# Two of the eight modulation products moved forward: into the first attention's seventh block and between two token tiles of the second attention's projections

## The chip, the cores and the metric

The kernel runs on one NeuronCore of a Trainium2 chip. The time is device microseconds (us) of one execution, from launch to the end of the output, and the number to predict is the median over several executions of the changed kernel. Beside it a profiled execution gives a trace, with the start and duration of every instruction on the five engines: TensorE (PE, with its weight loads as PEld), VectorE (DVE), ScalarE (ACT), GpSimd (POOL) and SyncE (SP, which issues nearly all DMAs).

## The reference

The program computes two transformer blocks on 512 tokens of width 1024. The first block has two attentions on the same input and a layer of 16 experts; the second has an mLSTM mixer and a gated convolution. Only the part around the change matters here:

```python
# first block, 512 tokens, D = 1024
o_a = window_gqa(q_a, k_a, v_a, rel_bias, sink)          # 8 heads, windows of 128 tokens
q  = rms_norm(c_q)  @ w_qb                                # 384 -> 8 x 96
kv = rms_norm(c_kv) @ w_kvb                               # 256 -> 8 x 128
o_b = softmax(q_nope k_nope + q_rot k_rot) v              # full attention, 8 heads
...
# second block: one row of 6 x 1024 numbers for c, one for c_ctx
mod   = silu(c)     @ w_mod + b_mod                       # w_mod is 1024 x 6144
mod_c = silu(c_ctx) @ w_mod + b_mod
```

The second block's modulation rows do not depend on the first block, so the kernel computes them while the first block's attentions run.

## The kernel before

**Order of work.** Every engine has one instruction stream written out by hand; engines wait for one another on semaphores (`wait_ge(*at(step, key))` waits for a named step, `then_inc(*inc(step, key))` marks it). Nothing is reordered by a planner.

**First attention.** It runs in eight blocks b = 0 to 7 (four blocks of 128 query tokens, two groups of heads). In the loop on TensorE block b does: the scores of block b+1 (`a_scores`, L520), for some blocks a modulation step (`mod_rows`, L530), the turning of block b's probabilities (L552, called At here), and the product with the values (L561, called Ao). The probabilities that At turns come from VectorE and ScalarE (exponential, L1167; scaling, L1649). "Seventh block" is b = 6.

**Second attention, front.** For each of four token tiles t TensorE makes the q projection (L574) and the kv projection (L580). ScalarE and VectorE follow tile by tile: copies out of PSUM (VectorE: L1663 for q, L1670 for kv), squares, norms, and the rotation, whose last instruction is L1060 and marks `qk` for the tile. Then TensorE waits for `qk` of tile 3, turns heads 0 and 1 (`b_heads`, L600), does the last modulation step, and begins the scores (`b_scores`, L433 to L435). ScalarE and VectorE split the turned heads in two parts (r_bh and r_bl, L1707).

**Modulation.** The product has K = 1024, cut in eight steps k of 128 rows. A step reads 128 x 6144 weights as two halves, so there are 16 loads m = 0 to 15 of 1536 KB each; `mod_rows(k)` waits for load 2k, does its six products, waits for load 2k+1 and does six more, and marks `pe_mod` after each half. The results of the eight steps are added up in three PSUM banks, which ScalarE copies out after `pe_mod` 15 (`modrow`, L1068), in front of its first exponential of the second attention (L1227).

The loads go into a ring of three buffers, so load m is issued by SyncE only when half m-3 has been multiplied (L2251, L2252):

```python
if m >= 3:
    sp.wait_ge(*at("pe_mod", m - 3))
sp.dma_start(w_mod[:, m % 3, :], ...)
```

Behind load 15 SyncE issues w_o (L2253), and after `pe_mod` 15 the first four expert loads (L2262).

Of the kernel before, what the change touches and what calls it, by code (L numbers as in the profile page):

```python
# [19 lines left out]
KD = D // P  # L20
# [72 lines left out]
class Marks:  # L93
# [14 lines left out]
    def inc(self, name, key=0, by=1):  # L108
        shared = SEM_OF.get(name, name)
        self.count[shared] = self.count.get(shared, 0) + by  # L110
        self.here[name, key] = self.count[shared]
        return self.sem(name), by

    def at(self, name, key=0):
        return self.sem(name), self.value(name, key)
# [37 lines left out]
def program(nc, I, out, known):  # L153
# [6 lines left out]
    with ctx:  # L160
# [31 lines left out]
        def bank(b, n=HALF):  # L192
            return PS[:, b * HALF:b * HALF + n]
# [220 lines left out]
        def _(pe):  # L414
# [10 lines left out]
            def nb(key, *freed_by, banks=8):  # L425
                b = turn[0] % banks
                turn[0] += 1
                bank_of[key] = claim(b, *freed_by)
                return b
# [12 lines left out]
            for t in range(NT):  # L442
                pe.wait_ge(*at(f"x_in{t}"))
                half, odd = divmod(t, 2)
                for k in range(KD):
                    b = 4 * half + k // 2
# [16 lines left out]
            for half in range(2):  # L463
# [5 lines left out]
                for k in range(KD):  # L469
# [13 lines left out]
                    for i in range(6):  # L483
                        t, c, kk = (i // 3, i % 3, k) if half == 0 else (2 + k // 4, (6 * (k % 4) + i) // 8, (6 * k + i) % 8)
# [8 lines left out]
            for j in range(10):  # L493
                freed = ("qT_" + "da"[j % 2], j) if j < 4 else ("kz", 3) if j == 4 else ("cT", j - 5)
                b = nb(("T", j), freed)
# [14 lines left out]
            def keys(n):  # L510
                return max(0, n - 1), min(NT - 1, n + 1)

            def a_scores(b):
                n, g = divmod(b, 2)
                lo, hi = keys(n)
                for i in range(4):
                    h = 4 * g + i
                    x = nb(("As", b, i), ("As", (b, i)), banks=5)
                    r = slice(64 * (h % 2), 64 * (h % 2) + 64)
                    pe.matmul(bank(x, (hi - lo + 1) * P), qTa[r, h // 2, n * P:(n + 1) * P],  # L520
                              kz[r, g, lo * P:(hi + 1) * P], start=True, stop=True).then_inc(*inc("pe_As", (b, i)))

            def mod_rows(k):

                for half in range(2):
                    m = 2 * k + half
                    pe.wait_ge(*at(f"w_mod{m % 3}", m))
                    for j2 in range(6):
                        r, j = divmod(6 * half + j2, 4)
                        mm = pe.matmul(PS[32 * j:32 * j + 32, (5 + r) * HALF:(6 + r) * HALF], csil[:, k, :],  # L530
                                       w_mod[:, m % 3, j2 * HALF:(j2 + 1) * HALF], start=(k == 0), stop=(k == KD - 1),
                                       skip_group_check=True)
                    mm.then_inc(*inc("pe_mod", m))
# [6 lines left out]
            for b in range(8):  # L540
                n, g = divmod(b, 2)
                lo, hi = keys(n)
                nk = hi - lo + 1
                if b < 7:
                    a_scores(b + 1)
                if b in (1, 2, 4, 5, 7):
                    mod_rows((1, 2, 4, 5, 7).index(b))
                for i in range(4):
                    x = nb(("At", b, i), ("ptA_" + "da"[i % 2], (b, i)), banks=5)
                    pe.wait_ge(*at("Ap", (b, i)))  # L550
                    for kk in range(nk):
                        tr = pe.transpose(bank(x)[:, kk * P:(kk + 1) * P], pA[:, 4 * (b % 2) + i, kk * P:(kk + 1) * P], ident)  # L552
                    tr.then_inc(*inc("pe_At", (b, i)))
                x = nb(("Ao", b), ("oTa", b), banks=5)
                for i0 in (0, 2):
                    for i in (i0, i0 + 1):
                        pe.wait_ge(*at("ptA_" + "da"[i % 2], (b, i)))
                    for kk in range(nk):
                        for i in (i0, i0 + 1):
                            o = PS[64 * (i % 2):64 * (i % 2) + 64, x * HALF + (i // 2) * P:x * HALF + (i // 2 + 1) * P]  # L560
                            mm = pe.matmul(o, zr[:, lo + kk, g * AD:(g + 1) * AD], ptA[:, i, kk * P:(kk + 1) * P],  # L561
                                           start=(kk == 0), stop=(kk == nk - 1), skip_group_check=True)
                mm.then_inc(*inc("pe_Ao", b))
# [6 lines left out]
            for t in range(NT):  # L570
# [6 lines left out]
                for c in range(2):  # L577
# [2 lines left out]
                        mm = pe.matmul(bank(x), cqT[:, 3 + k, t * P:(t + 1) * P], w_kvb[:, k, c * HALF:(c + 1) * HALF],  # L580
                                       start=(k == 0), stop=(k == 1))
                    mm.then_inc(*inc("pe_kv", (t, c)))
            for k in range(5, KD - 1):
                mod_rows(k)

            def turn_mod():

# [1783 lines left out]
```

## Time and profile before

| | us |
|---|---|
| median of 3 runs | 1560.69 |
| lowest and highest | 1559.26 and 1561.72 |
| the profiled execution: its time | 1559.61 |
| the profiled execution: its span in the trace | 1557.8 |

The span runs from the first to the last instruction in the trace; the execution's own time is 1.8 us more. Times in the rows below are counted from the start of the span. In the table of windows, PEclk is the TensorE clock that was granted as a share of full speed: 1.00 is 2.4 GHz and 0.50 is 1.2 GHz.

### The profile page before, as it was taken

Reading aid. Unit: us, or ns where it says so; the run is one execution under the profiler, and the core shown is the slowest. Engines: PE = TensorE matmul, PEld = TensorE weight load, DVE = VectorE, ACT = ScalarE, POOL = GpSimd, SP = SyncE. Lnnn points to the kernel's source line nnn. Section 1 sums busy time; section 2 is a strip of 40 time slices with the busy share of each in tenths; the row PEclk is TensorE's granted clock in tenths of the full one; section 3 lists DMA queues with packets and bytes.
Section 4 is the critical chain, followed back from the end, with each engine's and each line's share of the span. In section 5 each row is a group of like instructions: output and inputs, shape, how many; then the busy total and the mean of one; then the engine's idle time right before and its main releaser. Section 6 shows DMA issues by size and latency. Waiting matters only on the chain.

```text
span 1557.8 us, 17583 instructions
## 1 busy us (share of the span) xinstructions
PE 1459.2 (94%) x7133; PEld 956.3 (61%) x7133; DVE 616.2 (40%) x1188; ACT 490.8 (32%) x904; POOL 69.4 (4%) x96
## 2 busy tenths in 40 slices
PE   8988988998999999999996999988898999999998
PEld 6855466454433433333323899966686888888886
DVE  5366666334122222122115542125675443254325
ACT  6355376331001101100103412357734333123321
POOL 2000000000000000000001200000001101000100
PEclk9989999999999999999998999989999999999999
DMA  7477350427999999999995122140021332233211
GB/s 231 81 306 280 131 208 1 149 104 283 423 420 422 421 421 421 421 421 422 421 421 201 41 89 75 55 162 1 10 86 54 109 108 76 87 108 108 101 35 54
DMA packets 82738, 310.27 MB, mean 199 GB/s; under 512 B 7188, under 2 KB 43309, under 8 KB 55906
## 3 DMA queue, kind: packets, MB, share of 16 engines
q1 hardware_dynamic: 80656, 305.34, 50.2%
q10 hardware_dynamic: 1202, 2.15, 1.2%
q0 software_dynamic: 800, 1.66, 0.3%
q8 instruction: 57, 0.93, 0.2%
q14 instruction: 23, 0.19, 0.0%
HBM read 303.35 MB, written 5.78 MB: 198 GB/s over the span
## 4 chain that ended last, share of the span: by engine, by line
PE 73%; DMA 14%; DVE 6%; ACT 5%; issue 1%; SPq 0%; DVEq 0%; ACTq 0%
PE ps L433 13%; PE ps L434 13%; PE ps L435 13%; PE ps L805 13%; DMA sb<-in_w_gate 5%; DMA sb<-in_w_up 5%; PE ps L663 4%; DMA sb<-in_w_down 2%; PE ps L932 1%; PE ps L757 1%; DMA raw<-in_a_w_in 1%; ACT sb L1068 1%; PE ps L530 1%; PE ps L574 1%; PE ps L620 1%
## 5 line engine op out<-in xcount | busy, mean ns | idle before, releaser
L805 PE MATMUL ps<-sb 128*64 128x512 f32 x1536 | 352.5, 599 | 15.7 <-DMA sb<-in_w_gate 5.4
L805 PEld LDWEIGHTS ps<-sb 128*64 128x64 f32 x1536 | 102.9, 136 | 222.2 <-issue 178.6
L1068 ACT ACTIVATE sb<-ps 128x512 f32<-128x512 f32 (+4 forms) x176 | 90.7, 530 | 342.5 <-PE ps L757 88.3
L434 PE MATMUL ps<-r_fl,r_top 128*128 128x512 f32 x344 | 135.1, 393 | 0.0
L435 PE MATMUL ps<-r_act,r_low 128*128 128x512 f32 x344 | 134.8, 392 | 0.0
L433 PE MATMUL ps<-r_act,r_top 128*128 128x512 f32 x344 | 134.3, 390 | 0.0
L2096 DVE TENSOR_TENSOR r_low<-raw,r_top 128x2048 fp32r<-128x2048 f32 x33 | 74.2, 2289 | 78.7 <-ACT r_top L1068 78.7
L1874 DVE TENSOR_TENSOR sb<-sb,ps 128x512 f32<-128x512 f32 x64 | 43.7, 687 | 139.6 <-PE ps L794 139.6
L433 PE MATMUL ps<-r_low,r_h 128*128 128x256 f32 x288 | 82.5, 287 | 1.0 <-ACT sb L1068 1.0
L1068 ACT ACTIVATE r_top<-raw 128x2048 fp32r<-128x2048 f32 x33 | 61.4, 1907 | 69.7 <-PE ps L435 69.7
L434 PE MATMUL ps<-r_low,r_h 128*128 128x256 f32 x288 | 82.3, 286 | 0.0
L434 PE MATMUL ps<-r_low,r_mid 128*128 128x512 f32 x208 | 80.9, 389 | 0.0
L433 PEld LDWEIGHTS ps<-r_act,r_top 128*128 128x128 f32 x344 | 64.6, 188 | 14.7
L434 PEld LDWEIGHTS ps<-r_fl,r_top 128*128 128x128 f32 x344 | 64.6, 188 | 14.5
L435 PEld LDWEIGHTS ps<-r_act,r_low 128*128 128x128 f32 x344 | 64.6, 188 | 14.1
L435 PE MATMUL ps<-r_low,r_hl 128*128 128x256 f32 x256 | 73.2, 286 | 0.0
L1330 ACT ACTIVATE sb<-ps 128x512 f32<-128x512 f32 x16 | 9.6, 597 | 197.0 <-PE ps L805 197.0
L435 PE MATMUL ps<-r_top,r_mid 128*128 128x512 f32 x176 | 68.5, 389 | 0.0
L433 PE MATMUL ps<-r_top,r_mid 128*128 128x512 f32 x176 | 68.5, 389 | 0.0
L433 PEld LDWEIGHTS ps<-r_low,r_h 128*128 128x128 f32 x288 | 56.1, 195 | 1.8 <-issue 1.7
L663 PE MATMUL ps<-sb 128*128 128x512 f32 x128 | 56.3, 594 | 0.9 <-ACT sb L1068 0.9
L434 PEld LDWEIGHTS ps<-r_low,r_h 128*128 128x128 f32 x288 | 56.1, 195 | 0.0
(396 smaller groups left out, 2382.4 us busy)
## 6 DMA issues: line engine op xcount, KB each, us to landing
sb<-in_w_gate SPq DMA_DIRECT2D x64, 1024.0 KB, 25.3
sb<-in_w_up SPq DMA_DIRECT2D x64, 1024.0 KB, 26.0
sb<-in_w_down SPq DMA_DIRECT2D x64, 1024.0 KB, 26.4
sb<-in_w_mod SPq DMA_DIRECT2D x16, 1536.0 KB, 9.1
raw<-in_f_w_up SPq DMA_DIRECT2D x22, 1024.0 KB, 7.6
raw<-in_a_w_in SPq DMA_DIRECT2D x12, 1024.0 KB, 5.4
raw<-in_f_w_down SPq DMA_DIRECT2D x5, 2048.0 KB, 7.8
raw<-in_w_in SPq DMA_DIRECT2D x3, 1440.0 KB, 16.5
```

The source lines that it names most:

```text
L433: pe.matmul(o, a_hi, b_hi, start=first, stop=False)
L434: pe.matmul(o, a_hi, b_lo, start=False, stop=False)
L435: return pe.matmul(o, a_lo, b_hi, start=False, stop=last)
L530: mm = pe.matmul(PS[32 * j:32 * j + 32, (5 + r) * HALF:(6 + r) * HALF], csil[:, k, :], w_mod[:, m % 3, j2 * HALF:(j2 + 1) * HALF], start=( ...
L574: mm = pe.matmul(bank(x, 384), cqT[:, k, t * P:(t + 1) * P], w_qb[:, k, c * 384:(c + 1) * 384], start=(k == 0), stop=(k == 2))
L620: mm = pe.matmul(PS[64 * e:64 * e + 64, x * HALF:x * HALF + 256], vb[:, kk, h * VD:(h + 1) * VD], pT[g % 2][e][:, kk, :], start=(kk == 0), ...
L663: mm = pe.matmul(bank(x), oT[:, k, t * P:(t + 1) * P], w_o[:, k, hf * HALF:(hf + 1) * HALF], start=(k == 4 * part), stop=(k == 4 * part + 3))
L757: mm = pe.matmul(bank(6 + hf), onehot[:, t, :], part[t][:, hf * HALF:(hf + 1) * HALF], start=(t == 0 and part is h2hi), stop=(t == NT - 1 ...
L805: mm = pe.matmul(PS[64 * hf:64 * hf + 64, b * HALF:(b + 1) * HALF], lhsT(k), ring[c % RINGN][:, kk, hf * HALF:(hf + 1) * HALF], start=(k = ...
L1068: return act_(o, i_, ACT.Identity, bias=bias, scale=scale)
L1874: ve.tensor_tensor(o, o, bank(scatter_bank(i, n)), ALU.add).then_inc(*inc("x_add", (i, n)))
L2096: ve.tensor_tensor(w_lo(q, o, 2048), w_raw(q, o, 2048), w_hi(q, o, 2048).bitcast(F32), ALU.subtract).then_inc(*inc("wlo", (q, half)))
```

## The change

Steps k = 0 to 4 of the modulation stood in blocks 1, 2, 4, 5 and 7 of the first attention, and steps 5 and 6 behind the last projection. Now steps 0 to 5 stand in blocks 1, 2, 4, 5, 6 and 7, and step 6 stands behind the projections of token tile 1. Step 7 stays behind `b_heads`. The loads are the same and in the same order, and no other engine's code is changed.

```diff
-                if b in (1, 2, 4, 5, 7):
-                    mod_rows((1, 2, 4, 5, 7).index(b))
+                if b in (1, 2, 4, 5, 6, 7):
+                    mod_rows((1, 2, 4, 5, 6, 7).index(b))
...
                     mm.then_inc(*inc("pe_kv", (t, c)))
-            for k in range(5, KD - 1):
-                mod_rows(k)
+                if t == 1:
+                    mod_rows(6)
```

On TensorE, in block 6 of the first attention (L520 is here the scores of block 7, L552 and L561 the At and Ao of block 6, L530 a modulation step):

```order
 L561 MATMUL ps<-sb 64x128 x12
 L520 MATMUL ps<-sb 128x256 x4
+L530 MATMUL ps<-sb 32x512 x12
 L552 MATMUL ps<-sb 128x128 x8
 L561 MATMUL ps<-sb 64x128 x8
```

A step of twelve products, which is now k = 4, has come in between the scores of block 7 and the At of block 6; the step in block 7 stays in its place and is now k = 5.

On TensorE, in the projections of the second attention (L574 and L580 are the q and kv products of one token tile, L600 is `b_heads`; the rows begin with token tile 1):

```order
 L574 MATMUL ps<-sb 128x384 x6
 L580 MATMUL ps<-sb 128x512 x4
+L530 MATMUL ps<-sb 32x512 x12
 L574 MATMUL ps<-sb 128x384 x6
 L580 MATMUL ps<-sb 128x512 x4
 L574 MATMUL ps<-sb 128x384 x6
 L580 MATMUL ps<-sb 128x512 x4
-L530 MATMUL ps<-sb 32x512 x24
 L600 MATMUL ps<-sb 96x128 x16
 L530 MATMUL ps<-sb 32x512 x12
```

The 24 products of steps 5 and 6 have gone from between the last projection and `b_heads`; twelve of them, step 6, stand behind token tile 1.

## Rows read from the trace of the kernel before

**Rows 1.** The page: its span, and TensorE's busy time.

```profile
span 1557.8 us, 17583 instructions
PE 1459.2 (94%) x7133; PEld 956.3 (61%) x7133; DVE 616.2 (40%) x1188; ACT 490.8 (32%) x904; POOL 69.4 (4%) x96
```

**Rows 2.** Timeline of TensorE, blocks 6 and 7: start, length, instructions, idle before.

```profile
137.00 1.13 PE L520 MATMUL ps<-sb 64*128 64x256 f32 x8
140.53 1.20 PE L552 MATMUL ps<-sb 128*128 128x128 f32 x8 [2.39 <-DVE sb L1649]
142.13 1.98 PE L561 MATMUL ps<-sb 128*64 128x128 f32 x16 [0.40 <-DVE sb L1654]
144.03 3.36 PE L530 MATMUL ps<-sb 128*32 128x512 f32 x24
147.33 1.09 PE L552 MATMUL ps<-sb 128*128 128x128 f32 x8
```

**Rows 3.** SyncE: issues of loads 7 and 8, then of loads 9 and 10.

```profile
125.73 1.22 SPq L2252 DMA_DIRECT2D sb<-in_w_mod  x2
...
133.18 1.22 SPq L2252 DMA_DIRECT2D sb<-in_w_mod  x2
```

**Rows 4.** Time from issue to landing: loads 7 and 8 together; load 9; load 10.

```profile
DMA to landing us min/median/max: 6.2/7.6/9.1
...
DMA to landing us min/median/max: 8.5/8.5/8.5
...
DMA to landing us min/median/max: 11.2/11.2/11.2
```

**Rows 5.** Timeline of TensorE, from the projections to the scores of the second attention.

```profile
149.63 4.14 PE L574 MATMUL ps<-sb 128*128 128x384 f32 x12
...
179.04 4.49 PE L530 MATMUL ps<-sb 128*32 128x512 f32 x36
187.36 3.63 PE L530 MATMUL ps<-sb 128*32 128x512 f32 x12 [3.83 <-DMA sb<-in_w_mod]
190.91 2.97 PE L600 MATMUL ps<-sb 128*96 128x128 f32 x16
193.82 2.82 PE L530 MATMUL ps<-sb 128*32 128x512 f32 x24
196.57 0.50 PE L433 MATMUL ps<-r_bh,r_bh 96*128 96x512 f32 x1
```

**Rows 6.** SyncE: issue of loads 13 and 14; below it the landing of load 13.

```profile
181.00 1.22 SPq L2252 DMA_DIRECT2D sb<-in_w_mod  x2
...
DMA to landing us min/median/max: 6.3/6.3/6.3
```

**Rows 7.** Timeline of VectorE: tile 0's first copy, tile 2's copies, tile 3's last instruction.

```profile
153.81 0.56 DVE L1663 COPY sb<-ps 128x384 f32<-128x384 f32 x1 [2.60 <-PE ps L574]
...
172.01 0.55 DVE L1663 COPY sb<-ps 128x384 f32<-128x384 f32 x1
...
174.40 0.42 DVE L1670 COPY sb<-ps 128x256 f32<-128x256 f32 x1
...
188.69 0.28 DVE L1060 TENSOR_TENSOR sb<-sb 128x128 f32<-128x128 f32 x1
```

**Rows 8.** Windows of one us, columns as in the first line.

```profile
core 0: us, PE busy (x) PEld busy (x) DVE busy (x) ACT busy (x) POOL busy (x), PEclk, DMA share, GB/s
142.00:143.00 1.00, 0.87 (x8) 0.90 (x10) 1.00 (x2) 0.25 (x1) 0.00 (x0) 0.50 0.84 356
187.00:188.00 1.00, 0.64 (x4) 0.20 (x8) 0.97 (x5) 0.00 (x0) 0.00 (x0) 0.50 0.98 418
192.00:193.00 1.00, 1.00 (x7) 0.95 (x6) 0.24 (x1) 0.79 (x2) 0.00 (x0) 0.50 1.09 467
193.00:194.00 1.00, 1.00 (x12) 0.79 (x14) 0.89 (x2) 1.00 (x2) 0.00 (x0) 0.98 0.84 356
```

**Rows 9.** Timeline of ScalarE behind the last modulation step.

```profile
196.69 1.57 ACT L1068 ACTIVATE sb<-ps 128x512 f32<-128x512 f32 x3 [1.94 <-PE ps L530]
...
199.57 0.69 ACT L1227 ACTIVATE sb<-ps,sb 128x512 f32<-128x512 f32 x1
```

## The prediction, made before the changed kernel ran

> **What bounds the kernel now.** I read the page first: TensorE is busy 94% of a span of 1557.8 us [rows 1], so in most of the program what moves a TensorE instruction moves the end. Then I read the timeline of TensorE around the edit, the idle times in brackets above all, and for each idle time the engine that ended it. Two stretches matter. In block 6 the scores of block 7 end at 137.00 + 1.13 = 138.13, and TensorE is idle for 2.39 us until VectorE has scaled the probabilities [rows 2]. That looks like a free place for products. The second is the tail behind the projections: steps 5 and half of 6 begin at 179.04, then TensorE idles 3.83 us for load 13, which was issued only at 181.00, when the first half of step 5 was done, and landed 6.3 us later [rows 6], the second half of step 6 takes from 187.36 to 190.91, `b_heads` follows at 190.91, step 7 at 193.82, and the scores begin at 196.57 [rows 5]. ScalarE begins to copy the modulation rows at 196.69, when step 7 ends, and begins its first exponential only at 199.57 [rows 9]. So the end of step 7 releases the whole second attention, and everything behind it. I therefore follow that one moment, 196.57, and take its shift as the shift of the end.
>
> The third view is the clock. In the windows it stands at 0.50 (1.2 GHz) at 142, and again from 187 until it is back near 1.00 (2.4 GHz) at 193 [rows 8]; both times TensorE had been idle shortly before. The reader should see that the tail before costs not only the wait of 3.83 us: the half step behind it takes 190.91 - 187.36 = 3.55 us, and a whole step (24 records, two for each product) takes only 196.57 - 193.82 = 2.75 us at full clock [rows 5].
>
> **The change part by part.**
>
> *Removed from the tail.* Steps 5 and 6 took 190.91 - 179.04 = 11.87 us of TensorE's time, wait included [rows 5]. But this is not what is gained. `b_heads` also waits for the rotation of tile 3 on VectorE, which ends at 188.69 + 0.28 = 188.97 [rows 7]. So if nothing else moved, `b_heads` could start 190.91 - 188.97 = 1.94 us earlier and no more; with some 0.1 us for the signal, 1.8. The stall goes from a DMA to VectorE.
>
> *Step 4 in block 6.* It can start at 138.1. Its first half needs load 8, issued second in the pair at 125.73 and landed 9.1 us after its own issue, near 135.7 [rows 3, 4]: there. Its second half needs load 9, issued at 133.18 and landed 8.5 us later, at 141.7 [rows 3, 4]. So the free 2.39 us are spent mostly waiting for a load. The ring explains it: load 9 is issued when the first half of step 3 is multiplied, and nothing of the change makes that earlier. A half step on its own took 3.55 us at low clock, so I take half of that, 1.8 us, at full clock. At of block 6 starts at 141.7 + 1.8 = 143.5 at full clock and 145.2 at the low one, in place of 140.53. Ao follows 1.6 us later (142.13 - 140.53) and took 1.98 us, so block 6 ends between some 146.5 and 148.5, in place of 144.03 [rows 2].
>
> *Step 5 in block 7.* Load 10 was issued second of its pair, near 134.07, and landed 11.2 us later, at 145.3, that is 3.6 us behind load 9 [rows 3, 4]; it is there. Load 11 needs the first half of step 4, which now ends at about 139.9, so SyncE issues it near 140.3, behind loads 9 and 10 in a queue that is full. It lands one load's time after load 10: 145.3 + 3.7 = 149.0. The second half of step 5 then runs from 149.0 to 150.8. If block 6 ran late at low clock, the two halves run together and end about there too (147.8 + 2.75 = 150.6). At of block 7 started at 147.33 before [rows 2], so everything behind it starts 3.3 us later, 3.5 at most of this working. Here is the price: the step moved into a gap of 2.39 us waits for transfers that were not asked for early enough.
>
> On the price of a load there is a figure to weigh. The trace gives 3.6 to 3.8 us for 1536 KB in a full queue [rows 4]. The Trainium skill, "DMA: Bandwidth & Descriptors", section "Specifications", gives some 358 GB/s as the limit from HBM for one core; as an estimate from that page a load would take 4.4 us and load 11 land at 149.7, so the sum would be 0.7 us more. The row decides, and it is nearer to the page's other figure, 435 GB/s for the fabric.
>
> *Step 6 between tiles 1 and 2.* Its loads 12 and 13 are issued near 145 and 148 and land before 160 even by the slowest time of a load here, 11.2 us; step 6 starts near 149.63 + 3.3 + 2 x 7.35 = 167.6, since the four tiles took (179.04 - 149.63)/4 = 7.35 us each [rows 5]. It costs 2.75 us of TensorE at full clock. Does this delay VectorE, which now sets the end of this stretch? Its tile takes (172.01 - 153.81)/2 = 9.1 us in the mean of the first two [rows 7], TensorE's 7.35, so TensorE has run ahead. Tile 2's q products ended at 149.63 + 2 x 7.35 + 4.14 = 168.5 and VectorE took them at 172.01: 3.5 us of cover for 2.75. The kv products ended at 149.63 + 3 x 7.35 = 171.7 and VectorE took them at 174.40: 2.7 us of cover for 2.75, even. I take 0.1 us. Without that cover the step would cost its full 2.75.
>
> *The tail after.* VectorE's end moves with the start of the projections: 188.97 + 3.3 + 0.1 = 192.4, and `b_heads` starts near 192.5. TensorE is done with the projections near 179.04 + 3.3 + 2.75 = 185.1 and idles some 7.4 us, longer than the 3.83 us before, so the clock is low again when `b_heads` starts. `b_heads` took 2.91 us at low clock (193.82 - 190.91) and takes the same, until 195.4. Before, the clock rose at about 193, as step 7 began; now it will rise somewhere in step 7 or behind it. At full clock step 7 takes 2.75 us, at low clock 5.5. Before, TensorE had worked for 5.7 us (from 187.36 to the rise at 193.0) when the clock rose [rows 5, 8]; the low stretch at 142 was over after less. If it rises at 196.5, step 7 ends at 198.7; after 5.7 us, at 198.2, it ends at 199.6; if not in time, at 200.9. Against 196.57 that is +2.1, +3.0 and +4.3. I take +2.4, between the first two.
>
> *Else.* SyncE issues w_o near 170 and not at 184, in an idle queue, and nobody waited for it; I count nothing. The expert loads behind `pe_mod` 15 move with it. The sum, at the end of step 7: 1.94 us of the tail's 11.87 can be kept (-1.94), blocks 6 and 7 cost +3.3, VectorE +0.1 and the signal +0.1, which puts `b_heads` 1.56 us later; the clock in step 7 costs a further +0.84. Net +2.4 us: 1557.8 + 2.4 = 1560.2 of span. The execution's own time is 1.8 us above its span and 1.1 us below the median, so on the median 1560.69 + 2.4 = 1563.1; I say 1563.0.
>
> **Bounds.** Low: if loads 9 to 11 follow load 8 without the slip (135.7 + 3 x 3.7 = 146.8), the second half of step 5 ends at 148.9 by its own work before it, the shift there is 1.6 us, and with the clock rising early step 7 ends at 188.97 + 1.7 + 2.9 + 2.75 = 196.3, -0.2 us. High: TensorE's idle in blocks 6 and 7 brings a low stretch just when load 11 is in. Before, such a stretch cost Ao and step 4 about 0.9 and 0.6 us; 1.5 more, with step 7 wholly at low clock, gives 4.3 + 1.5 = +5.8 us. To both I add some half us for the spread of the three runs.
>
> **The rivals.** A change of 0.2%, 3.1 us, is about what a measurement of this kernel can tell from none.
>
> Forecast, 0.66: the waits for loads 9 and 11 eat the gap, VectorE takes over the tail, and it ends at +0.5 to +3.1 us (1561.2 to 1563.8).
>
> Slower, 0.28, the other side: the clock. Its place is step 7, its price is up to 2.75 us, and it decides if the clock rises later than some 5.8 us after `b_heads` starts: then step 7 ends behind 199.7, more than 3.1 us late. For it speaks the rise before after 5.7 us of work, and an idle time twice as long; against it that the rise at the first low stretch came sooner. It gives 1564 to 1566.5. The Trainium skill, "TensorE: Matmul & The Clock Gate", section "What's actually happening", says that the low clock is the default, that activity releases it, and that the chip looks on a schedule of its own that does not start with the kernel. By that rule a longer idle before `b_heads` speaks against this change, and the place of the rise differs between executions. The trace agrees so far that both low stretches follow idle times; no row here shows the schedule.
>
> The change does what its name promises, 0.06: load 11 lands early, the delay in block 7 is 1.6 us or less, and the clock is high in half of `b_heads`, which saves 1.4 of its 2.91 us. Then step 7 ends at 188.97 + 1.7 + 1.5 + 2.75 = 194.9, -1.6 us: 1559.1, and only with luck elsewhere below 1557.6, 0.03 of it. Against it stands VectorE's 188.97, which the edit can't move forward.
>
> It changes nothing: the tail's gain and blocks 6 and 7 cancel within half a us; this is the forecast's low end, and it is counted there and in the case above.
>
> **How the numbers follow.** Slower by more than 0.2%: 0.28. Faster by more: 0.03. The rest, 0.69, within. The range of 8 in 10 runs from 1560.0 (the low bound with the spread of the runs) to 1566.5 (the high bound).
>
> **What the changed profile would show.** In block 6 TensorE waits some 2 us in front of L530 for w_mod, in place of VectorE's 2.39 us. In block 7 a second wait for w_mod, or none if block 6 ran at low clock, and the projections start near 153. The wait for load 13 is gone, and a wait of about 7 us for VectorE stands before L600, which starts near 192.5; ScalarE's copies of the modulation rows start at 198.5 to 201. I am wrong if the projections start before 151.5 (load 11 is faster than the queue says), if L600 starts more than 3.5 us behind the projections' own shift (step 6 starves VectorE), or if stretches far behind the edit move by more than this shift.

## The result and the profile after

The changed kernel takes 1565.15 us in the median of 20 runs (1560.67 to 1569.16), the kernel before 1561.25 us in 20 runs beside them. The ratio is 1.0024, with a 95% interval of 1.0017 to 1.0032: slower by 3.9 us, a little more than the 0.2% that I had called the limit of a measurement. It lies inside the range of 1560.0 to 1566.5, 2.15 us above the value given; 0.56 us of this is the kernel before, whose median is 1561.25 over 20 runs and was 1560.69 over three.

The page has the same number of instructions as before [rows 1], and 3.6 us more span:

```profile
span 1561.4 us, 17583 instructions
PE 1458.0 (93%) x7133; PEld 954.9 (61%) x7133; DVE 616.3 (39%) x1188; ACT 491.4 (31%) x904; POOL 67.5 (4%) x96
```

TensorE is busy a little less (1458.0 us against 1459.2) in a longer span, so over the whole span the loss is waiting; a busy time also holds what a low clock adds, and low stretches differ from profile to profile, as shown further on. Timeline of TensorE in the changed kernel, from the scores of block 7 to the scores of the second attention; it answers to [rows 2, 5]:

```profile
136.80 1.13 PE L520 MATMUL ps<-sb 64*128 64x256 f32 x8
137.86 1.91 PE L530 MATMUL ps<-sb 128*32 128x512 f32 x12
141.74 3.33 PE L530 MATMUL ps<-sb 128*32 128x512 f32 x12 [1.97 <-DMA sb<-in_w_mod]
145.01 1.31 PE L552 MATMUL ps<-sb 128*128 128x128 f32 x8
146.51 1.09 PE L561 MATMUL ps<-sb 128*64 128x128 f32 x16 [0.19 <-ACT sb L1068]
147.53 3.49 PE L530 MATMUL ps<-sb 128*32 128x512 f32 x24
150.95 1.09 PE L552 MATMUL ps<-sb 128*128 128x128 f32 x8
...
153.25 4.14 PE L574 MATMUL ps<-sb 128*128 128x384 f32 x12
...
168.06 2.78 PE L530 MATMUL ps<-sb 128*32 128x512 f32 x24
...
193.01 3.65 PE L600 MATMUL ps<-sb 128*96 128x128 f32 x16 [7.37 <-DVE sb L1060]
196.59 2.81 PE L530 MATMUL ps<-sb 128*32 128x512 f32 x24
199.32 0.50 PE L433 MATMUL ps<-r_bh,r_bh 96*128 96x512 f32 x1
```

Read the brackets first. The idle time of block 6 is still there, 1.97 us, but it now ends with a load and not with VectorE, and it stands in the middle of step 4. Step 5 hides its wait inside a stretch: 24 records take 3.49 us in place of 2.8. The wait of 3.83 us for load 13 is gone from the tail, and 7.37 us for VectorE stand there.

SyncE's issues of loads 9 and 11, each with its time to landing below it:

```profile
132.97 0.33 SPq L2252 DMA_DIRECT2D sb<-in_w_mod  x1
...
DMA to landing us min/median/max: 8.7/8.7/8.7
...
139.81 0.33 SPq L2252 DMA_DIRECT2D sb<-in_w_mod  x1
...
DMA to landing us min/median/max: 9.2/9.2/9.2
```

Load 9 lands at 141.7 and load 11 at 149.0, the two moments that hold TensorE. VectorE, which answers to [rows 7]:

```profile
157.43 0.56 DVE L1663 COPY sb<-ps 128x384 f32<-128x384 f32 x1 [2.59 <-PE ps L574]
...
175.63 0.55 DVE L1663 COPY sb<-ps 128x384 f32<-128x384 f32 x1
...
178.38 0.42 DVE L1670 COPY sb<-ps 128x256 f32<-128x256 f32 x1 [0.27 <-PE ps L580]
...
192.67 0.28 DVE L1060 TENSOR_TENSOR sb<-sb 128x128 f32<-128x128 f32 x1
```

The first copy is 3.62 us later than before and the last rotation 3.98, so VectorE's own stretch has grown by 0.36 us. Between them stands a wait of 0.27 us for tile 2's kv products, behind step 6; before, this copy had no wait in front of it. The windows of one us show the clock, as [rows 8] did:

```profile
189.00:190.00 1.00, 0.00 (x0) 0.00 (x0) 0.68 (x4) 0.22 (x1) 0.00 (x0) 0.93 0.00 0
195.00:196.00 1.00, 1.00 (x6) 0.96 (x5) 0.90 (x2) 0.83 (x2) 0.00 (x0) 0.50 0.00 0
196.00:197.00 1.00, 1.00 (x8) 0.40 (x10) 0.89 (x2) 0.83 (x2) 0.00 (x0) 0.65 0.00 0
197.00:198.00 1.00, 1.00 (x16) 0.31 (x12) 0.89 (x2) 0.38 (x1) 0.00 (x0) 1.00 0.00 0
```

It fell just before 190, ahead of `b_heads`, stayed at 0.50 through it, and rose at 196.7, as step 7 began.

Profiles of one kernel begin this stretch at times that differ by up to 1.9 us, though nothing in front of it was edited. So I count from the start of the scores of block 7 (137.00 before [rows 2], 136.80 after): to the projections 12.63 us before and 16.45 after (+3.82), to `b_heads` 53.91 and 56.21 (+2.30), to the scores of the second attention 59.57 and 62.52 (+2.95).

One thing must be known before the tables are read. In front of the projections the kernel before and four of the experiments have the same code in the same order, and yet their profiles need 12.63, 12.18, 11.16, 12.62 and 11.17 us to the projections. The difference is the clock in blocks 6 and 7. With step 4 in block 7 and the same idle time of 2.39 us, this profile (of the split steps, below) has no low stretch there: Ao takes 1.09 us where it took 1.98 [rows 2], and the step 2.78 where it took 3.36.

```profile
140.90 1.20 PE L552 MATMUL ps<-sb 128*128 128x128 f32 x8 [2.39 <-DVE sb L1653]
...
143.53 2.78 PE L530 MATMUL ps<-sb 128*32 128x512 f32 x24
```

So up to 1.5 us in the column of the projections, and in every column behind it, is this clock and no effect of an edit. What the tail does by itself is read from the projections to `b_heads`, which the table gives as a column of its own.

### The profile page after: what moved, and what is told of

Same layout as the page of the kernel before. It is cut to its first block, busy times and chain, and to the rows that moved or that the text cites. A ratio compares the mean times of both kernels' runs of the same rounds, so it can differ in the third digit from the quotient of the medians.

```text
span 1561.4 us, 17583 instructions
## 1 busy us (share of the span) xinstructions
PE 1458.0 (93%) x7133; PEld 954.9 (61%) x7133; DVE 616.3 (39%) x1188; ACT 491.4 (31%) x904; POOL 67.5 (4%) x96
## 3 DMA queue, kind: packets, MB, share of 16 engines
q10 hardware_dynamic: 1202, 2.15, 1.2%
## 4 chain that ended last, share of the span: by engine, by line
PE 71%; DMA 16%; DVE 6%; ACT 5%; issue 1%; SPq 0%; DVEq 0%; ACTq 0%
PE ps L433 13%; PE ps L434 13%; PE ps L435 13%; PE ps L805 11%; DMA sb<-in_w_gate 7%; DMA sb<-in_w_up 5%; PE ps L663 4%; DMA sb<-in_w_down 2%; PE ps L932 2%; DMA raw<-in_a_w_in 1%; PE ps L757 1%; ACT sb L1068 1%; PE ps L620 1%; PE ps L530 1%; PE ps L574 1%
```

## The experiments

My theory: in blocks 6 and 7 TensorE waits for loads that the ring asks for too late; VectorE takes over the tail, so the wait that goes there brings 1.9 us at most; and the longer idle time in front of `b_heads` keeps the clock low. The rivals: the placement between the tiles costs, or the 2.75 us of products ahead of the projections themselves. Three columns of the table are us from the scores of block 7 in each profile, the fourth is the time from the projections to `b_heads`, and the last is the ratio to the kernel before with its 95% interval.

| kernel | projections | b_heads | scores | projections to b_heads | ratio |
|---|---|---|---|---|---|
| before | 12.63 | 53.91 | 59.57 | 41.28 | 1 |
| changed | 16.45 | 56.21 | 62.52 | 39.76 | 1.0024 (1.0017 to 1.0032) |
| changed, again | 16.06 | 55.80 | 62.09 | 39.74 | 1.0023 (1.0011 to 1.0035) |
| tiles only | 12.18 | 51.94 | 58.07 | 39.76 | 0.9982 (0.9972 to 0.9992) |
| blocks only | 16.00 | 55.40 | 61.56 | 39.40 | 1.0012 (1.0000 to 1.0025) |
| light loads | 11.18 | 50.95 | 57.49 | 39.77 | 0.9988 (0.9975 to 1.0000) |
| busy gap | 15.75 | 55.52 | 60.11 | 39.77 | 1.0001 (0.9989 to 1.0013) |
| ring of four | 12.29 | 52.04 | 58.78 | 39.75 | 0.9987 (0.9974 to 0.9999) |
| ring of four, step 7 early | 12.31 | 52.06 | 57.35 | 39.75 | 0.9985 (0.9974 to 0.9997) |
| split steps | 11.16 | 51.82 | 56.09 | 40.66 | 0.9980 (0.9970 to 0.9990) |
| tiles only, busy | 12.62 | 52.38 | 56.97 | 39.76 | 0.9983 (0.9974 to 0.9993) |
| split steps, rows first | 11.17 | 51.83 | 54.73 | 40.66 | 0.9993 (0.9983 to 1.0004) |

**Tiles only: no step in block 6.**

```diff
-                if b in (1, 2, 4, 5, 6, 7):
-                    mod_rows((1, 2, 4, 5, 6, 7).index(b))
+                if b in (1, 2, 4, 5, 7):
+                    mod_rows((1, 2, 4, 5, 7).index(b))
...
-                if t == 1:
-                    mod_rows(6)
+                if t in (1, 3):
+                    mod_rows(5 + t // 2)
```

> The blocks of the first attention are as in the kernel before (step 4 in block 7), and steps 5 and 6 stand behind token tiles 1 and 3 of the projections. Theory (the price of the change is paid in blocks 6 and 7, by waits for loads 9 and 11): projections start at 149.6 as before; load 11 lands near 153 and load 13, asked for near 166, near 172, so no half step waits; VectorE's last rotation ends near 189.0, b_heads starts at 189.1 with some 4 us of idle time before it, the clock is low in it, and the scores start near 195 to 196 (196.57 before, 199.32 in the changed kernel). Time about 1 to 2 us below the kernel before. Rival (the placement between tiles itself costs): VectorE's end moves by 2 us or more and the time is that of the changed kernel, +2 to +4.

Measured 1559.3 us, ratio 0.9982. TensorE's timeline of the tail:

```profile
149.05 4.14 PE L574 MATMUL ps<-sb 128*128 128x384 f32 x12
...
188.81 3.48 PE L600 MATMUL ps<-sb 128*96 128x128 f32 x16 [4.67 <-DVE sb L1060]
192.23 2.78 PE L530 MATMUL ps<-sb 128*32 128x512 f32 x24
194.94 0.50 PE L433 MATMUL ps<-r_bh,r_bh 96*128 96x512 f32 x1
```

That is 2.8 us below the kernel before, more than the 1 to 2 expected. No wait for a load is left. `b_heads` starts 1.97 us earlier than before by the table, but 0.45 of it is already there at the projections, where nothing was edited: the clock in block 6. The tail itself gained 1.52 us (41.28 to 39.76), of the 1.94 that VectorE's end allows. The steps between the tiles are therefore not free, as the next run shows. With the blocks left alone the kernel is faster than before; with them edited, and a ring of three, it is slower.

**Blocks only: step 6 behind the last tile.**

```diff
-                if t == 1:
+                if t == 3:
                     mod_rows(6)
```

> Steps 0 to 5 in blocks 1, 2, 4, 5, 6, 7 as changed, step 6 behind the last projection and not between tiles 1 and 2. Theory: projections start at 153.2 as in the changed kernel, VectorE's last rotation ends 0.3 us earlier than there (192.7 against 192.95, since the kv products of tile 2 are no longer late), step 6 ends near 185.7 and b_heads waits some 7 us for VectorE all the same; time that of the changed kernel within 0.5 us, +3 to +4 on the kernel before. Rival (step 6 between the tiles is the cost): 2 to 3 us faster than the changed kernel.

Measured 1564.26 us, ratio 1.0012: 1.9 us above the kernel before, where 3 to 4 was expected. That is below the changed kernel's 1.0024 by 1.9 us, nearly the rival's 2 to 3, but the intervals overlap and the times can't decide it. Both waits for loads stand open here, since the clock stayed high in block 6:

```profile
142.77 1.91 PE L530 MATMUL ps<-sb 128*32 128x512 f32 x12 [1.38 <-DMA sb<-in_w_mod]
...
150.26 1.91 PE L530 MATMUL ps<-sb 128*32 128x512 f32 x12 [1.43 <-DMA sb<-in_w_mod]
...
193.81 3.51 PE L600 MATMUL ps<-sb 128*96 128x128 f32 x16 [7.21 <-DVE sb L1060]
```

The projections come 3.37 us late and `b_heads` 1.49, so in the profile nearly all of the price is there without the placement between the tiles. What that placement adds stands in the column from the projections to `b_heads`: 39.40 us here, and 39.74 to 39.77 in the eight profiles in which one whole step stands behind tile 1 and none behind tile 2. It costs 0.36 us, not the rival's 2 to 3.

**Light loads: loads 9, 10 and 11 cut to a quarter.**

```diff
-                sp.dma_start(w_mod[:, m % 3, :], wm[:, m // 2, (m % 2) * 3072:(m % 2 + 1) * 3072])...
+                n = 768 if m in (9, 10, 11) else 3072
+                sp.dma_start(w_mod[:, m % 3, 0:n], wm[:, m // 2, (m % 2) * 3072:(m % 2) * 3072 + n])...
```

> The changed kernel with loads 9, 10 and 11 cut to a quarter of their columns (384 KB in place of 1536 KB), so these weights are left out of the result; same products, same order, same waits. Theory (the loads are late): no wait for w_mod in blocks 6 and 7 beyond 0.5 us, the At of block 6 starts near 140.7 and the projections start at 148.5 to 149.5 in place of 153.25; b_heads starts near 188.5 to 189 and the scores near 195; time 3 to 5 us below the changed kernel, at or just below the kernel before. Rival (the products themselves, 2.75 us more of TensorE's work ahead of the projections, are the price): projections start at 152 or later and the time stays 2 us or more above the kernel before.

Measured 1560.79 us, ratio 0.9988. Blocks 6 and 7 with the same products and quick loads:

```profile
139.15 2.78 PE L530 MATMUL ps<-sb 128*32 128x512 f32 x24
...
144.24 2.78 PE L530 MATMUL ps<-sb 128*32 128x512 f32 x24
```

The rest of these weights is left out; the products are all there. Both steps take their plain 2.78 us with no idle time, and the projections start 5.3 us earlier than in the changed kernel (11.18 against 16.45). They also start 1.45 us earlier than in the profile before, but that is the clock again: the two profiles of the unedited blocks without a low stretch stand at 11.16 and 11.17. Against those, a whole step more in the gap costs nothing. So the products themselves are not the price; the gap in block 6 would have hidden step 4 if its load had been there. The time is below the changed kernel by 0.0036 of 1561, 5.6 us, a little more than the 3 to 5 expected.

**Busy gap: eight products of no use in front of b_heads.**

```diff
+            x = turn[0] % 5
+            for m in owner.get(x, ()):
+                pe.wait_ge(*at(*m))
+            for _ in range(8):
+                pe.matmul(bank(x), ident, w_qb[:, 0, 0:HALF], start=True, stop=True)
             pe.wait_ge(*at("qk", 3))
```

> The changed kernel with eight extra products of 512 columns (ident by w_qb into the PSUM bank that b_heads takes next; their result is overwritten) in the idle time before b_heads, 6.9 us of work in 7.4 us. Theory (part of the price is the low clock behind that idle time): the clock stays at 1.00 through b_heads and step 7, b_heads takes 2.1 us in place of 3.58, the scores start near 197.9 in place of 199.32, and the time is 1.5 us below the changed kernel, more if in most of its executions the clock rises only within step 7. Rival (the clock in this place costs nothing that lasts): the time is that of the changed kernel within 0.5 us.

Measured 1562.34 us, ratio 1.0001. TensorE's timeline and, in a second fence, the window around it:

```profile
186.05 7.03 PE L636 MATMUL ps<-sb 128*128 128x512 f32 x16
193.59 1.95 PE L600 MATMUL ps<-sb 128*96 128x128 f32 x16 [0.51 <-DVE sb L1065]
195.47 2.78 PE L530 MATMUL ps<-sb 128*32 128x512 f32 x24
198.18 0.50 PE L433 MATMUL ps<-r_bh,r_bh 96*128 96x512 f32 x1
```

```profile
186.00:195.00 9.00, 8.49 (x30) 4.27 (x29) 5.95 (x18) 2.57 (x7) 0.00 (x0) 1.00 0.03 8
```

The same 16 turnings take 1.88 us until step 7 (193.59 to 195.47) in place of 3.58 (193.01 to 196.59), and the clock is 1.00 throughout. So work added in a wait makes the kernel faster, here by 1.70 us from `b_heads` to step 7 (the 2.41 us at the scores include 0.70 from in front of the projections). The ratio falls by 0.0023, 3.6 us, with an uncertainty of some 2 us, and the two intervals don't meet; the low clock in this place costs 1.7 us in the profile, and the times agree with that or more.

**Ring of four: the loads asked for half a step earlier.**

```diff
-        w_mod = sb(0, 3, 3072)
+        w_mod = [SB[:, o:o + 3072] for o in (0, 3072, 6144, W_O)]
...
-                if m >= 3:
-                    sp.wait_ge(*at("pe_mod", m - 3))
+                if m >= 4:
+                    sp.wait_ge(*at("pe_mod", m - 4))
...
+            sp.wait_ge(*at("pe_mod", 15))
             sp.dma_start(w_o, ...)
```

> The changed kernel with a ring of four buffers for the loads in place of three (the fourth lies where w_o goes later, so w_o is loaded after step 7); nothing is left out. Theory (loads 9 and 11 are late because they are asked for late): load 9 is asked for near 126 and lands near 136, load 11 is asked for near 134 and lands before 146; no wait of more than 0.5 us in blocks 6 and 7; from the scores of block 7 to the scores of the second attention it takes 57 to 58 us, as with the light loads (57.5), in place of 62.5; time 2 us below the kernel before. Rival (the queue is full in this stretch and an earlier request lands no earlier): load 11 lands near 149 again, and the time is that of the changed kernel.

Measured 1560.11 us, ratio 0.9987. SyncE's issues of loads 9 and 11 and their landing:

```profile
126.66 0.33 SPq L2252 DMA_DIRECT2D sb<-in_w_mod  x1
...
DMA to landing us min/median/max: 9.1/9.1/9.1
...
134.10 0.33 SPq L2252 DMA_DIRECT2D sb<-in_w_mod  x1
...
DMA to landing us min/median/max: 11.0/11.0/11.0
```

Load 9 lands at 135.8 and load 11 at 145.1, 6 and 4 us earlier than in the changed kernel, and the projections start 4.2 us earlier. The rival (a full queue, so no earlier landing) falls: asked for 6.3 us earlier, load 9 also lands 5.9 us earlier, so it was the ring and not the queue that had made it late. For load 11 the queue takes a part back: asked for 5.7 us earlier, it needs 11.0 us in place of 9.2 and lands 3.9 earlier. Step 5 therefore still waits: it took 3.90 us (143.19 to 147.03), 1.1 more than the plain 2.78 and more than the half us that I had allowed. The stretch to the scores took 58.78 us where I expected 57 to 58; the rest of the difference is step 7, which took 3.16 us since the clock rose only within it, 4.5 us behind the start of `b_heads`. The time is 2.0 us below the kernel before, as expected. The edit also moves w_o behind step 7, which was not tried by itself.

**Ring of four with step 7 in front of b_heads.**

```diff
                 if t == 1:
                     mod_rows(6)
+                if t == 3:
+                    mod_rows(7)
...
             b_heads(1, banks=5)
-            mod_rows(KD - 1)
```

> Ring of four as in the run beside it, steps 4 and 5 in blocks 6 and 7 and step 6 behind tile 1 as changed, and step 7 behind tile 3 in place of behind b_heads. Theory: projections start near 149.5 or earlier, VectorE's end is not late by more than 0.1 us, TensorE idles some 4.5 us before b_heads, which starts near 189 at low clock (3 to 3.6 us); the scores start 4 us earlier than before, at 192 to 193; time 4 to 5 us below the kernel before, the fastest of all. Rival (ScalarE's chain behind b_heads takes over): only 2 to 3 us below.

Measured 1559.79 us, ratio 0.9985: 2.3 us below and not 4 to 5; 2 to 3 was the rival's. TensorE's timeline and, in a second fence, the windows show two causes:

```profile
195.66 0.77 PE L433 MATMUL ps<-r_bh,r_bh 96*128 96x512 f32 x1 [1.65 <-DVE r_bl L1708]
```

```profile
190.00:191.00 1.00, 0.63 (x3) 0.61 (x4) 0.31 (x2) 0.00 (x0) 0.00 (x0) 0.50 1.01 410
...
194.00:195.00 1.00, 0.01 (x1) 0.00 (x0) 0.89 (x2) 0.95 (x2) 0.00 (x0) 0.50 1.02 410
...
202.00:203.00 1.00, 1.00 (x9) 0.85 (x8) 1.00 (x3) 0.22 (x1) 0.00 (x0) 0.96 0.99 410
```

With step 7 gone from behind `b_heads`, TensorE idles a second time, at 194, for 1.65 us until VectorE has split the turned heads: that much of the rival is true. And the clock stays at 0.50 until 202, so the first fifteen products of the scores, from 195.66 to the turning at 202.14, take 6.5 us where the changed kernel needs some 3.7. By the scores this kernel is 2.2 us ahead of the one before, by the first turning only 0.4.

**Split steps: all of the modulation in front of b_heads, with the old ring.**

```diff
-            for k in range(5, KD - 1):
-                mod_rows(k)
+                if t == 1:
+                    mod_rows(5)
+                if t == 2:
+                    mod_rows(6, (0,))
+                if t == 3:
+                    mod_rows(6, (1,))
+                    mod_rows(7)
...
             b_heads(1, banks=5)
-            mod_rows(KD - 1)
```

The edit is against the kernel before; the second argument of `mod_rows` picks the halves.

> Blocks of the first attention as before (step 4 in block 7); step 5 behind token tile 1, the first half of step 6 behind tile 2, its second half and all of step 7 behind tile 3, so nothing of the modulation stands behind b_heads any more. Theory (step 7 is on the path only because it stands behind b_heads, and the idle time before b_heads lowers the clock): projections start at 149 to 149.6, load 15 is asked for near 176.5 and lands near 183, TensorE is done with step 7 near 188; VectorE's last rotation is 0.5 to 1 us late (189.5 to 190), because 4.65 us of work stand before tile 3's kv products and only 3.8 are covered; b_heads starts near 190 at full clock, and the scores start near 193, 3.5 us earlier than before (196.57). Time 3 to 4.5 us below the kernel before. Rival (ScalarE's row copies and table load are the bound, whatever TensorE does): the first exponential moves by less than 2 us and so does the time.

Measured 1560.1 us, ratio 0.9980, 3.1 us below the kernel before.

```profile
182.90 4.49 PE L530 MATMUL ps<-sb 128*32 128x512 f32 x36
189.20 1.95 PE L605 MATMUL ps<-sb 128*96 128x128 f32 x16 [1.81 <-DVE sb L1064]
193.47 0.47 PE L433 MATMUL ps<-r_bh,r_bh 96*128 96x512 f32 x1 [2.31 <-DVE r_bl L1711]
...
198.58 0.60 PE L649 MATMUL ps<-sb 128*128 128x128 f32 x4
```

The scores start 3.48 us earlier, of which 1.47 are the clock in blocks 6 and 7, where nothing was edited, and 2.01 the tail. A wait of 2.31 us that step 7 had covered comes to light in front of them, and behind it the clock is low from 194 to 198. The rival is out: the first exponential comes 4.8 us earlier (57.81 us behind the scores of block 7 in place of 62.57).

**Split steps, rows copied first, scores from bank 5.**

```diff
-            b_q(0)
-            b_q(1)
             for r in range(3):
                 eng.wait_ge(*at("pe_mod", 15))
                 copy(modrow[:, r, :], bank(5 + r))...
+            b_q(0)
+            b_q(1)
...
+            turn[0] = 5
             for u in range(4):
                 b_scores(u)
```

> The kernel of the split steps (nothing of the modulation behind b_heads), where the first scores started only at 193.47, 2.3 us after b_heads, behind the last of VectorE's four r_bl parts. Two edits: ScalarE copies the modulation rows ahead of its parts of heads 0 and 1, and the scores begin at PSUM bank 5 in place of bank 4. Theory (the first scores took the bank in which the last turned head still lay, a wait that step 7 covered before): the scores start 1 to 1.5 us earlier against the start of b_heads (2.9 us behind it in place of 4.3), the first turning of probabilities about 1 us earlier, and the time is 0.5 to 1 us below the split steps, 3.5 to 5 below the kernel before. Rival (the scores wait for the heads themselves): no change against the split steps.

Measured 1560.06 us, ratio 0.9993.

```profile
189.10 1.95 PE L605 MATMUL ps<-sb 128*96 128x128 f32 x16 [1.82 <-DVE sb L1065]
192.00 0.47 PE L433 MATMUL ps<-r_bh,r_bh 96*128 96x512 f32 x1 [0.95 <-DVE r_bl L1712]
...
195.79 0.63 PE L650 MATMUL ps<-sb 128*128 128x128 f32 x4
...
212.86 1.05 PE L634 MATMUL ps<-sb 128*128 128x1 f32 x8 [1.99 <-ACT sb L1232]
```

The mechanism was as expected: the scores start 2.9 us behind `b_heads` in place of 4.3, and the first turning follows at 195.79, 6.7 us behind `b_heads` in place of 9.4. But nothing of it lasts. A wait of 1.99 us stands in front of `out_squares` (L634), which takes the fixed bank 7, and behind it the clock is at 0.50 from 215 to 218, which costs some 1.6 us more; the whole is no faster than the split steps. That the new order of banks makes this wait is read from the code and wasn't tried by itself.

**Tiles only with five such products in the gap** (the busy gap's edit with `range(5)`).

> The kernel of the tiles only (steps 5 and 6 behind token tiles 1 and 3), with five extra products of 512 columns (ident by w_qb, overwritten later) in the 4.66 us of idle time before b_heads. Theory (the low clock behind that idle time costs what b_heads takes more than 2 us): b_heads starts near 188.8 as without them, takes 1.95 us in place of 3.4, the scores start near 193.5 in place of 194.9, and the time is 1.5 us below the tiles only, some 3 to 5 us below the kernel before. Rival (the clock's price here is not kept to the end): the same time as the tiles only.

Measured 1558.94 us, ratio 0.9983 against 0.9982 without them. At the scores the gain is there, 1.10 us by the table (56.97 against 58.07; the projections came 0.44 later in this profile); in the times it isn't, though the intervals would allow 1 us. The profiles hold one hint. Both kernels with products of no use have a low stretch near 240 that costs 1.65 us, and neither of the kernels that they were made from has it. The kernel before has it too, with no such products, so this is no proof, and it stays open.

**The changed kernel again.**

> The changed kernel once more, beside the others on the same chip. Loads 9 and 11 land near 141.7 and 149 again and the projections start at 153 to 154; the clock is low in b_heads and may rise up to 2 us later or earlier than in the first profile, which would move the start of the scores against the end of b_heads' wait by as much; time 3 to 5 us above the kernel before.

Measured 1565.88 us, ratio 1.0023. The projections 3.43 us late, the scores 2.52. A second run gives the same loss by the same stations.

## Why the prediction was right, and where it was off

*Blocks 6 and 7, +3.3.* Right in kind and nearly in size: +3.82 and +3.43 in two profiles. Load 11 landed at 149.0, as forecast. The light loads and the ring of four show the cause, each in its way. But the profile before was among the slow ones of its own code (12.63 us to the projections, 11.95 in the mean of five profiles of the same code), while the four profiles with step 4 in block 6 and late loads stand at 15.75 to 16.45, 16.07 in the mean. By the means the price is 4.1 us, 0.8 above the forecast, which counted from a profile with this low stretch in it, though its upper bound shows that it had seen the stretch (0.9 and 0.6 us).

*VectorE takes over the tail, 1.94 us at most.* Right: the tiles only gained 1.52 us in the tail, and the 0.36 of the next point is the rest but for the signal. In the changed kernel the wait is 7.37 us where 7.4 was forecast, and `b_heads` starts at 193.01 where 192.5 was.

*Step 6 between the tiles, 0.1.* It cost 0.36 us, at L1670, where the cover of 2.7 us for 2.75 had pointed. The step moves TensorE's work by 2.91 us and not 2.75 (tile 2's kv products end 25.09 us behind the start of the projections in place of 22.18).

*The clock.* Mis-sized in two parts that nearly cancel. `b_heads` took 3.58 us and not 2.91: the 2.91 had been taken from a stretch at whose end the clock had already risen. Step 7 took 2.73 us and not 3.6, since the clock rose as it began, 3.7 us behind the start of `b_heads`. Together 6.3 us where 6.5 was forecast. So the rival of the clock, a rise more than 5.8 us behind the start of `b_heads`, is not what either profile shows, although the time came out on its side of 0.2%; that the low clock costs something here is shown by the busy gap. That the clock can stay low longer is shown by the ring of four with step 7 in front of `b_heads`, where it rose 11.7 us behind the start of `b_heads`, with an idle time in between.

*The sum.* +2.4 was forecast for the scores, +2.95 and +2.52 were found, and the whole kernel lost 3.9 us (interval 2.7 to 5.0). Following one moment was a fair method: in ten of the eleven rows of the table the shift at the scores and the shift of the time agree within 1.4 us (the last row, -4.84 against -1.1, is the exception, with the wait at L634). Part of the 1 us that is missing here is the choice of profiles: by the means the projections come 4.1 us late, and from there to the scores the changed kernel is 0.9 us quicker than the profile before (46.07 and 46.03 us against 46.94), which gives an estimate of 3.2 us, inside the interval; the rest stays open. But a single profile can't be followed to its end. The sign of being wrong that I had named, stretches far behind the edit that move by more than this shift, did come true in part, and in two places it is seen to be the clock. The windows from 240 to 245, before and then changed:

```profile
240.00:245.00 5.00, 5.00 (x26) 4.40 (x25) 2.81 (x8) 2.54 (x6) 0.00 (x0) 0.66 0.01 3
...
240.00:245.00 5.00, 3.04 (x21) 2.69 (x22) 2.81 (x8) 3.51 (x9) 0.00 (x0) 1.00 0.01 3
```

The low stretch of the kernel before is not in the changed one, and the shift falls there from 3.0 to 1.4 us. From 370 to 378 it is the other way, a granted clock of 0.79 before and 0.57 after, and the shift rises from 0.6 to 2.1; at the end it is 3.9. So it is luck that the span of this profile grew by nearly what the medians show. The value given, 1563.0, is 2.15 us low, and the likeliest case, "within 0.2%", was missed by a small margin: the chance of 0.28 for slower was too small for a forecast that itself lay so near the limit. The upper bound of 1566.5 is 1560.69 + 5.8 without the half us for the spread of the runs that the text adds to both bounds; with it, it would be 1567.0.

*The Trainium skill's rule* on the clock (the Trainium skill, "TensorE: Matmul & The Clock Gate", "What's actually happening": the low clock is the default and activity releases it) did speak against this change, and the traces agree: with the gap filled the clock stays at 1.00 and `b_heads` takes 1.88 us. The forecast also had the place of the rise differ between executions, and between these profiles it does: 3.2 us behind the start of `b_heads` in the tiles only, 3.7 in the changed kernel, 4.5 in the ring of four. The estimate from 358 GB/s (the Trainium skill, "DMA: Bandwidth & Descriptors", "Specifications") put load 11 at 149.7; it landed at 149.0, as the spacing of the loads in the trace had it.

## What to carry to other kernels

An idle time is free for moved work only if the operands of that work are there: look up when each transfer is issued and by what, and follow the ring backwards, since a step moved one place forward asks for loads that no earlier step releases. Before a wait is removed from a tail, look for the second condition of the same instruction; here it allowed 1.9 of 11.9 us. The better change was smaller: leave the first attention alone and put the steps between the tiles, 2.8 us faster than before. And before a gain is given to an edit, look whether it is already there in front of the edit: here the same code took 11.16 to 12.63 us.

## What was not expected of the hardware

A load issued into an empty queue lands 6.1 to 6.6 us after its issue in these profiles (load 13: 6.3 [rows 6]), but load 9, issued 2.5 us before load 8 landed, took 8.5 us before [rows 4] and 8.7 after. It landed 6 us behind load 8, where load 10, asked for earlier against its forerunner, lands 3.7 us behind load 9. And the same code with the same wait of 2.39 us finds the clock low in block 6 in one profile (before: Ao took 1.98 us) and high in another (split steps: 1.09 us). It is so in the changed kernel too: in its first profile the clock was low there (the half step took 3.33 us), in its second it was not (1.91 us). What decides it no run here shows.
